# Probabilities times values turned round in a one-core encoder step: split values stationary, split probabilities of 256 queries moving

## What is computed

```python
def sink_attention(q, k, v, bias, mask, sink):            # 8 heads, 2 key/value heads, window of 3 chunks of 64
    s = jnp.einsum('nqkgd,nskd->nkgqs', q, k) * SCALE + bias
    m = jnp.maximum(jnp.max(s, axis=-1, keepdims=True), sk)
    p = jnp.exp(s - m)
    p = p / (jnp.sum(p, axis=-1, keepdims=True) + jnp.exp(sk - m))
    return jnp.einsum('nkgqs,nskd->nqkgd', p, v)

def fox_attend(q, k, v, cq, ck, q_pos, k_pos):            # 8 heads, causal, c = cumsum(log sigmoid(forget logits))
    s = jnp.einsum('bqhd,bshd->bhqs', q, k) * SCALE + cq[..., :, None] - ck[..., None, :]
    s = jnp.where(k_pos[None, :] <= q_pos[:, None], s, NEG)
    return jnp.einsum('bhqs,bshd->bqhd', jax.nn.softmax(s, axis=-1), v)

def merge_and_ffn(x, ya, yb, ga, gb, w_oa, w_ob, w_out, g_ffn, w_gu, w_down):
    merged = jax.nn.sigmoid(ga) * (ya @ w_oa) + jax.nn.sigmoid(gb) * (yb @ w_ob)
    x = x + merged @ w_out
    a, u = jnp.split(rmsnorm(x, g_ffn) @ w_gu, 2, axis=-1)
    return x + (jax.nn.silu(a) * u) @ w_down
```

## Time and profile before

| | us |
|---|---|
| median of three runs | 1628.39 |
| span of the profiled execution | 1626.6 |
| sliding-window stage | 115.9 to 344 |
| forgetting stage | 344 to 607 |
| sample units | 607 to 721 |
| merge and w_out, group 0 | 721 to 812 |
| the rest | 812 to 1626.6 |

### The profile page before, as it was taken

The page is one execution under the profiler, slowest core; times in us unless marked ns, Lnnn a source line. Parts: engine busy times, 40 slices in busy tenths (PEclk is TensorE's granted clock), DMA queues, the critical chain, the costliest instruction groups (busy, mean ns, idle before and its releaser), DMA issues.

```text
span 1626.6 us, 27813 instructions
## 1 busy us (share of the span) xinstructions
PE 1600.6 (98%) x10614; PEld 1507.4 (93%) x10614; DVE 1021.5 (63%) x2232; ACT 665.0 (41%) x1333; POOL 175.3 (11%) x312
## 2 busy tenths in 40 slices
PE   8999999999999999999999999999999999999997
PEld 8999999999999999988898899999999999888886
DVE  6646555655546554436366677776677777679865
ACT  6335444544445444334253552222222223434453
POOL 3011111000000001012011000000121222110000
PEclk9999999999999999999999999999999999999999
DMA  7152332553341425759455332332344444776432
GB/s 210 29 168 95 128 105 68 186 172 93 119 146 52 123 93 152 218 171 326 146 172 193 123 93 93 107 105 75 91 149 157 158 158 165 253 235 187 143 128 87
DMA packets 190292, 230.60 MB, mean 142 GB/s; under 512 B 14808, under 2 KB 140281, under 8 KB 189641
## 3 DMA queue, kind: packets, MB, share of 16 engines
q1 hardware_dynamic: 163616, 138.71, 28.9%
q0 software_dynamic: 26544, 90.12, 15.6%
HBM read 166.76 MB, written 62.08 MB: 141 GB/s over the span
## 4 chain that ended last, share of the span: by engine, by line
PE 91%; DVE 6%; issue 2%; ACT 1%; DMA 1%; SPq 0%; DVEq 0%; ACTq 0%
PE ps L2261 25%; PE ps L2262 24%; PE ps L2263 24%; PE ps L2371 6%; PE ps L2326 3%; PE ps L2344 3%; PE ps L2565 1%; PE ps L2564 1%; DVE sprob L1560 1%; PE ps L2390 1%; DVE e_lo L1911 1%; PE ps L2409 0%; PE ps L2397 0%; PE ps L2283 0%; PE ps L2383 0%
## 5 line engine op out<-in xcount | busy, mean ns | idle before, releaser
L2261 PE MATMUL ps<-h_hi,w_hi 128*128 128x384 f32 (+1 forms) x816 | 274.1, 336 | 1.4 <-DVE h_lo L1532 1.4
L2263 PE MATMUL ps<-h_hi,w_lo 128*128 128x384 f32 (+1 forms) x816 | 266.3, 326 | 0.0
L2262 PE MATMUL ps<-h_lo,w_hi 128*128 128x384 f32 (+1 forms) x816 | 266.2, 326 | 0.0
L2261 PE MATMUL ps<-t_hi,e_hi 128*128 128x272 f32 x704 | 202.7, 288 | 0.9 <-DVE silu L1926 0.9
L2262 PE MATMUL ps<-t_lo,e_hi 128*128 128x272 f32 x704 | 202.8, 288 | 0.0
L2263 PE MATMUL ps<-t_hi,e_lo 128*128 128x272 f32 x704 | 202.1, 287 | 0.0
L2261 PEld LDWEIGHTS ps<-h_hi,w_hi 128*128 128x128 f32 x816 | 153.6, 188 | 3.5 <-DVE h_lo L1532 1.6
L2261 PE MATMUL ps<-b_hi,e_hi 128*128 128x272 f32 x528 | 152.5, 289 | 2.3 <-DVE silu L1926 1.1
L2262 PEld LDWEIGHTS ps<-h_lo,w_hi 128*128 128x128 f32 x816 | 153.5, 188 | 0.5 <-issue 0.5
L2263 PEld LDWEIGHTS ps<-h_hi,w_lo 128*128 128x128 f32 x816 | 153.2, 188 | 0.0
L2262 PE MATMUL ps<-b_lo,e_hi 128*128 128x272 f32 x528 | 152.1, 288 | 0.0
(11 more groups left out here) (340 smaller groups left out, 3620.9 us busy)
## 6 DMA issues: line engine op xcount, KB each, us to landing
w_raw<-in_w_gu_dram SPq DMA_DIRECT2D x104, 256.0 KB, 3.4
w_raw<-in_w_in_dram SPq DMA_DIRECT2D x68, 256.0 KB, 3.3
zg_d<-stg POOLq DMA_DIRECT2D x28, 544.0 KB, 3.0
act_d<-act POOLq DMA_DIRECT2D x44, 272.0 KB, 2.7
s_d<-s_sum POOLq DMA_DIRECT2D x44, 256.0 KB, 3.0
f_raw<-s_d SPq DMA_DIRECT2D x44, 256.0 KB, 2.8
f_raw<-act_d SPq DMA_DIRECT2D x33, 256.0 KB, 2.9
w_raw<-in_w_out_dram SPq DMA_DIRECT2D x32, 256.0 KB, 3.5
```

The source lines that it names most:

```text
L2261: nc.tensor.matmul(out, l_hi, r_hi, start=start, stop=False)
L2262: nc.tensor.matmul(out, l_hi, r_lo, start=False, stop=False)
L2263: return nc.tensor.matmul(out, l_lo, r_hi, start=False, stop=stop)
```

## The change

In `outputs` the operands change sides. The values of a block become the stationary one, high and low part side by side in 128 columns (`va_stack`, `vb_stack`). The turned probabilities become the moving one, high and low part in two products, for two units at once (a **duo**): in the sliding window the two heads of a pair, in the forgetting stage two neighbouring tiles of one head, which is why units 72 to 135 are now ordered by head (`head_start`) and keys, queries, forget sums and values are loaded and split per head. The result lies turned already, rows 0 to 63 of the high values, 64 to 127 of the low values; it is copied by ScalarE (`outputs_out`) and stored to `o_d`, a DMA per duo. Nothing is normalised in the stream: the row sums are kept, inverted once per stage, turned, stored (`rinv_a_d`, `rinv_b_d`) and loaded as rows broadcast over partitions. At the merge's load, per 128 columns of a group's half, VectorE adds the two row halves, multiplies by 1/sum, ScalarE casts and VectorE subtracts. The sample units keep the old form. The sink's exponential is now taken once for all units.

Step n on ScalarE is exp(n+1), evacuation, high part of **all** groups of n, high parts of turned and new things, copy of the duo's outputs (even n); on VectorE the rest of all groups of n, scores(n+2), low parts. TensorE sends outputs of units n-3 and n-2 at odd steps n. Cut to its core (new buffers' places, renamed semaphores and the per-head loads are left out):

```diff
-            def outputs(n):
...
-                for blk, val in enumerate(u["v"]):
-                    K = val.shape[0]
-                    p0 = turned_at(u) + blk * R
-                    last = nc.tensor.matmul(ps[0:R, out_bank(n), 0:w], probT[0:K, p0:p0 + R], val, start=blk == 0, stop=blk == nb - 1)
+            def outputs(m):
+                u, w = units[2 * m], units[2 * m + 1]
+                R, bank = u["rows"], out_bank(m)
+                hi, lo = turned_parts(u)
+                pe.wait_ge(pt_lo, w["group1"])
+                if m >= 2:
+                    pe.wait_ge(ot_evac, m - 1)
...
+                for blk, val in enumerate(w["v"]):
+                    K = val.shape[0]
+                    x0 = 0 if blk < len(u["v"]) else 1
+                    out = ps[:, bank, R * x0:2 * R].rearrange("p (x r) -> p x r", r=R)
+                    nc.tensor.matmul(out, val, hi[0:K, blk, x0:2, 0:R], start=blk == 0, stop=False)
+                    last = nc.tensor.matmul(out, val, lo[0:K, blk, x0:2, 0:R], start=False, stop=blk == len(w["v"]) - 1)
+                last.then_inc(o_ready, 1)
...
+            def turned_hi_part(n):                       # ScalarE
+                for g in range(u["group0"], u["group1"]):
+                    a.wait_ge(pt_ready, g + 1)
+                    for hi, _, src in group_views(u, g):
+                        ins = nc.scalar.copy(hi, src)
+                    ins.then_inc(pt_hi, 1)
+            def outputs_out(m):
+                a.wait_ge(o_ready, m + 1)
...
+                nc.scalar.copy(ost[:, m % 2, 0:w], ps[:, out_bank(m), 0:w]).then_inc(ot_evac, 1)
+            def merged_in_hi(g, part, k):
+                a.wait_ge(sem("ab_scaled"), 4 * (2 * g + part) + k + 1)
+                nc.scalar.copy(rooms[g][("ab_a", "ab_b")[part]][:, 0, k, 0:w], rooms[g][f"raw{part}"][:, 1, k, 0:w])
...
+            def turned_lo_part(n):                       # VectorE
+                for g in range(u["group0"], u["group1"]):
+                    v.wait_ge(pt_hi, g + 1)
+                    for hi, lo, src in group_views(u, g):
+                        ins = nc.vector.tensor_tensor(lo, src, hi.bitcast(F32), ALU.subtract)
+                    ins.then_inc(pt_lo, 1)
+            def merged_in_scale(g, part, ks_):
...
+                for k in ks_:
+                    nc.vector.tensor_tensor(raw[:, 1, k, 0:w], raw[:, 1, k, 0:w], raw[:, 0, k, 0:w], ALU.add)
+                for x, k in enumerate(ks_):
+                    nc.vector.tensor_tensor(raw[:, 1, k, 0:w], raw[:, 1, k, 0:w], r[:, k, 0:w], ALU.mult)
+            def merged_in_lo(g, part, k):
...
+                nc.vector.tensor_tensor(dst[:, 1, k, 0:w], rooms[g][f"raw{part}"][:, 1, k, 0:w], dst[:, 0, k, 0:w].bitcast(F32), ALU.subtract)
...
             for n in range(N_STREAM):                    # VectorE
-                empty_groups(v, nc.vector.tensor_copy, 1, units[n])
+                turned_lo_part(n)
...
-                if n >= 1:
-                    normalise(n - 1)
...
                 evac(d + 1)                              # ScalarE, sample unit s = 3
+                    for k in range(2, 4):
+                        merged_in_hi(0, 0, k)
+                    for k in range(4):
+                        merged_in_hi(0, 1, k)
                 evac(d + 2)
...
                 normalise(N_STREAM + s)                  # VectorE, sample unit
+                if s == 3:
+                    merged_in_scale(0, 1, (0, 1, 2, 3))
+                    for k in range(4):
+                        merged_in_lo(0, 1, k)
...
             def out_first():                             # VectorE; ScalarE has merged_in_hi after each split_hi
+                def chunk(c):
+                    split_lo(b + c + 1, (c + 1) % 2)
+                    merged_in_scale(1, c // 4, (c % 4,))
+                    if c:
+                        merged_in_lo(1, (c - 1) // 4, (c - 1) % 4)
```

More of the change, by code:

```diff
@@ L109 @@
 N_UNITS = 140
+N_SWA = 72
+N_DUOS = N_STREAM // 2
 def rows_of(t):
@@ L116, in pair_start, with head_start @@
 def pair_start(p):
-    return 18 * p if p < 4 else 72 + 16 * (p - 4)
+    return 18 * p
+def head_start(h):
+    return N_SWA + 8 * h
 def is_tok(n):
@@ L148, in bank_of, with out_bank, stat_col @@
     return p % 4 if p < 8 else p % 2
-def out_bank(n):
-    return 1 if n < N_STREAM and n % 2 else 6
+def out_bank(m):
+    return 1 if m % 2 else 6
+def stat_col(u):
+    return 18 * u["pair"] + 9 * u["e"] + u["t"] if u["kind"] == "swa" else u["n"]
 def product_bank(name, f):
@@ new lines, in load_pair, with load_head, load_keys_queries @@
+                saved_block(B_QA + p)
+                load_twice(qz[s], B_QA + p, slice(0, T), f"q_landed{s}")
+            def load_head(dst, n, e, name):
+                saved_block(n)
+                for half in range(2):
+                    sp.dma_start(dst[64 * half:64 * half + 64, :], zg_d[n, 64 * e:64 * e + 64, 0:SEQ]).then_inc(sem(name), 16)
+            def load_keys_queries(h):
+                s, i, e = h % 2, h // 2, h % 2
+                sp.wait_ge(s_ready, units[pair_start(3) - 1 if h == 0 else head_start(h - 1) - 1]["piece1"])
+                load_head(kz[s], B_KB + i, e, f"k_landed{s}")
+                load_head(qfz[s], B_QB + i, e, f"q_landed{s}")
@@ L1099, in turned_hi @@
+            def merged_in_hi(g, part, k):
+                w = 512 if part else GROUPS[g][3]
+                a.wait_ge(sem("ab_scaled"), 4 * (2 * g + part) + k + 1)
+                nc.scalar.copy(rooms[g][("ab_a", "ab_b")[part]][:, 0, k, 0:w], rooms[g][f"raw{part}"][:, 1, k, 0:w]) \
+                    .then_inc(sem("ab_hi"), 1)
             def turned_hi(ev):
-                if ev[0] == "tok":
+                if ev[0] in ("tok", "rinv"):
                     return
                 a.wait_ge(misc_ready, turn_index[ev] + 1)
-                if ev[0] == "ot":
-                    u = units[ev[1]]
-                    R, t, p = u["rows"], u["t"], u["pair"]
-                    if p and t in (0, 4):
-                        a.wait_ge(sem(f"ab_saved{t // 4}"), 32 * p)
-                    ins = nc.scalar.copy(ot_hi[:, P * t:P * t + R], ps[:, 7, 0:R])
-                elif ev[0] == "cache":
+                if ev[0] == "cache":
@@ L1197, in _ @@
             exp(0)
+            a.wait_ge(sem("s_prep_evac"), 3)
+            a.wait_ge(sem("swa_cache_landed"), 32)
+            for rows, blocks in ((slice(0, P), slice(0, NPT + 1)), (slice(0, DEC), slice(NPT + 1, NPT + 2))):
+                nc.scalar.copy(va_stack[rows, blocks, :, 0:HD], va_tok[rows, blocks, :].rearrange("p j (k d) -> p j k d", k=2)) \
+                    .then_inc(sem("v_hi_done"), 1)
             evac(16)
@@ L1205, in _ @@
                     evac(p)
-                empty_groups(a, nc.scalar.copy, 0, units[n])
+                turned_hi_part(n)
                 for ev in turns_at[n]:
@@ L1585, in normalise @@
-                if u["kind"] == "new":
-                    for h in range(2):
-                        rows = slice(64 * h, 64 * h + 64)
-                        ins = nc.vector.tensor_scalar(o_tok[rows, tl, 0:HD], ps[rows, 6, HD * h:HD * h + HD], rinv[rows, c],
-                                                      None, ALU.mult)
-                else:
-                    ins = nc.vector.tensor_scalar(o_tok[0:R, tl, HD * e:HD * e + HD], ps[0:R, out_bank(n), 0:HD], rinv[0:R, c], None,
-                                                  ALU.mult)
@@ L2368, in outputs, with outputs_new @@
+            def outputs_new(s):
+                u = units[N_STREAM + s]
+                for g in range(u["group1"] - 2, u["group1"]):
+                    pe.wait_ge(*emptied(g))
+                if s:
+                    pe.wait_ge(o_evac, s)
+                else:
+                    pe.wait_ge(ot_evac, N_DUOS)
+                pe.wait_ge(sem(f"vc_landed{s % 2}"), 32 * (s // 2 + 1))
                 for blk, val in enumerate(u["v"]):
                     K = val.shape[0]
-                    p0 = turned_at(u) + blk * R
```

587 lines of the change are left out of this document (352 added, 235 removed).

## The result

The changed kernel takes **1615.97 us** (1614.44 to 1616.70, four runs) against 1628.27 for the kernel before beside it: a ratio of 0.9921, with a 95% interval of 0.9907 to 0.9935. It is faster, by 12.3 us, where 40.4 were forecast, and it lies outside the range of 1573 to 1608. The profiled execution took 1614.44 us, its span 1612.5, which is 14.1 less than the 1626.6 of the span before.

What follows compares the result with a forecast made beforehand. TensorE was taken to bound the kernel (busy 98% of the span). Gains of 54.1 us less losses of 13.7 gave 40.4 us off, so a span of 1586.2 and a predicted 1588 us, range 1573 to 1608.

Steps and rivals of the forecast that it cites:

- The products: TensorE, sliding-window and forgetting stages: fp32r products of paired units cost 53.2 us instead of 89.5, gaining 36.3 us.
- Rival 4: TensorE's new products are slower than the score products, e.g. 0.2 us per wide one: 1618 us; chance 0.04.
- The turned outputs: TensorE, sliding-window and forgetting stages: 68 output transposes go, two of 1/sum come, gaining 8.3 us.
- the vanished wait: TensorE no longer waits for an output transpose's bank to empty before turning key or value tiles: 9.5 us gained.
- relay: Per-unit chain through ScalarE and VectorE (exp, evacuation, high copy, rest, scores): loses 3 us in forgetting, 1 in sliding window.
- start: Sliding-window start: ScalarE puts two copies of the values ahead of one evacuation, losing 0.5 us (0 to 1.5).
- cache tiles: Cache tiles turned in steps 130, 132, 133, 134, and first sample scores ahead of last outputs: 1 us lost (0 to 2).
- the mark of a wrong prediction: Signs named beforehand: wide products over 0.13 us apart, TensorE standing over 1 us a head, or pre-merge pause over 9 us.
- The join: Before merge(0): half b's loads land hidden, but the last evacuation stands behind four high copies; 5.2 us lost (3 to 9).
- The clock: TensorE after the stop before merge(0): a slower clock costs 1.5 us (0 to 2.8).
- Group 1's loads: GpSimd's queue carries 6.8 MB instead of 4.6 beside w_out's late weight chunks: 1.5 us lost (0 to 5).
- Rival 2: Loads bound the end: group 0's halves and group 1's loads land late, 5 us each: 1598 us; chance 0.1.

Runs made afterwards that it cites:

- no_sums: The changed kernel without the loads of the sums, so 1/sum is left out of the output: 1604.2 us.
- before_halves: The kernel before, with each load of the merge inputs cut into two DMAs, one per half of the partitions: 1639.9 us.
- combined: The changed kernel with last evacuation before half b's high parts, w_hi behind high copies, outputs loaded into 128 partitions, sums in small loads alternating partition halves: 1594.3 us.

## Why the prediction was wrong, point by point

**The products: right.** Of the 456 fp32r products 440 stand between 116 and 566 us and the last pair's 16 behind, and wide ones start 0.12 us apart, after 0.17 for the first of a unit:

```profile
519.89 0.33 PE L2571 MATMUL ps<-pb_hi,vb_stack 128*128 128x256 f32 x1
520.06 0.28 PE L2572 MATMUL ps<-pb_lo,vb_stack 128*128 128x256 f32 x1
520.18 0.28 PE L2571 MATMUL ps<-pb_hi,vb_stack 128*128 128x256 f32 x1
```

Added up from start to start, the products cost 90.8 us before (89.5 in the prediction, whose 27 for the 272 passes of the first stage should be 26.5 by its own row; they measure 28.2) and 54.2 for the 440 after; with the last 16 at the same price the gain is 34.7 us, where 36.3 were forecast. The narrow ones came at 0.115 each, for the 0.11 taken. Rival 4 is out.

**The turned outputs and the vanished wait: right.** No wait of the key and value turns (L2605, L2607) is left in the groups of 116 to 566 us, and the sliding-window stage came out at 204.6 us for the 203 named; its gross terms, 11.3 + 4.7 + 9.5 = 25.5, less the measured 23.5, leave 2.0 lost, for 1.5 forecast (relay 1, start 0.5).

**The relay: right in kind, too small.** The forgetting stage took 244.8 us instead of 237: 28.6 gross less 18.2 is 10.4 lost, for 4 forecast with the cache tiles. The loads of VectorE and ScalarE were read rightly (143.6 and 145.9 us busy, for 142 and 152). The loss lies between the named ends of 0 and 16, and TensorE stood for more than the 1 us a head that I had set as the mark of a wrong prediction: 8.5 us of waits in eight heads, 12.1 from start to start. The step that failed is the averaging: I put w_hi at 1.4 us into the sum of a head and took a stall of 0.4 for the rest. But it is one item of 1.04 us, and in the units where it comes, it stands ahead of the copy that empties one of two banks. Moving it gave 6.2 us; what is left of the 10.4, 4.2, is near the 4 that I had forecast.

**The join: the order right, the landing wrong.** VectorE came to half b at 678.3 us; by the prediction 720.1 less the 41.7 gained, 678.4. The evacuation behind four high copies costs 5.0 us (a stop of 5.6 in no_sums, less the 0.6 that the kernel before had), for 5.2 forecast. What failed is "landed 15 us after issue, hidden". I took the rate of the earlier trace rows, 2 MB in 9.8 us, for loads of another shape. They landed 22.0 us after the first issue, 5.8 after VectorE got there, and TensorE's stop was 5.8 us longer than by the order alone (11.4 against 5.6); the pause passed the 9 us named as wrong.

**The clock: right after this stop, left out after the later ones.** The stop had a granted clock of 0.67 on average; the first products of merge(0) after it:

```profile
690.74 0.63 PE L2466 MATMUL ps<-ab_a,w_hi 128*128 128x512 f32 x1
691.16 0.63 PE L2467 MATMUL ps<-ab_a,w_lo 128*128 128x512 f32 x1
```

They start 0.43 us apart instead of 0.23, half speed (the 1.2 GHz level), for some six products: 1.3 us, for 1.5 forecast. The rule of the Trainium skill that the prediction cites, "TensorE: Matmul & The Clock Gate", section "HAM oscillation — how this bites in real kernels", is borne out in kind: after this stop the next products ran at half clock. The upper end of 2.8 us at which the prediction put the cost by it was not reached. The prediction had one stop only; w_out has three more, of 4.77, 1.14 and 4.78 us, and the clock after them was put at nothing.

**Group 1's loads: the term that was mis-sized, and the largest.** 1.5 us (0 to 5) were forecast and 15.7 came. Of these 10.7 are waits for w_lo, and the other 5.0 go with slower products (the three lines' means are 424, 412 and 408 ns instead of 389), since after its long stops TensorE runs at half clock (0.50 from 745 to 750 us and 0.66 from 770 to 775; 0.91 over the stage). Rival 2, "the loads bound the end", was the right one, at a chance of 0.1, with its price for w_out again too small (5 us for each place; at the join the landing cost 5.8): it counted 2.2 MB more and not that all 6.8 MB go at about 60% of the rate. before_halves shows the width alone, with 4.6 MB, to be worth 10.2 us in this place. Not all of the 15.7 is width: combined, where the outputs go into 128 partitions and the sums take the halves in turn, still loses 6.2 there. The argument against that rival, "asked for 15 us or more ahead", was about latency, where the question was throughput: loads that fill the engines delay whoever shares them.

The sum again with what was measured: 54.1 - 2.0 - 10.4 - 10.7 - 1.2 - 15.7 = 14.1, the 14.1 of the spans. The 2.0 and the 10.4 are what the gross gain of each stage leaves over, so the sum closes by its making; that the gross gain stood within 2 us is shown by the products added up above. The losses were 40 us instead of 13.7.

## What to carry to other kernels

When a change re-shapes a transfer, price it by its own shape: count the partitions that each DMA writes and its outermost dimension, and take the rate from a row of such a load, not from the megabytes of another. Where the DMA engines are near full, ask whose loads share them; a wait in order for one landing may be harmless while the bytes are not, even when the chain names it. And in a strict queue put work with slack (a weight split, a load's unpacking) behind the copy that frees a bank, since a mean load of an engine hides what one item costs at the wrong place.

## What the runs showed of the hardware that was not expected

- Loads into 64 partitions hold all 16 DMA engines full at 206 GB/s (2 KB packets) or 237 to 254 GB/s (mixed with other loads), where 128 partitions gave 325 to 412. Small ones that take the halves in turn reached 303 GB/s at 93% from SyncE's queue, but 274 at 104% from GpSimd's.
- A load whose outermost dimension is 2 ran on 13.0% of the engines, at 50 GB/s, from SyncE's queue; from GpSimd's it did not stay there.
- Reading one DRAM row for 64 partitions costs no more than reading 64 rows (226 and 223 GB/s while the sums load).
- TensorE's clock can fall after the engine has started again. In combined it stood for 2.71 us, did four products at full rate, and then fell to half (granted clock by stretch, 736 to 739, 739 to 740 and 740 to 743 us), which cost another 1.5 us or so:

```profile
736.00:739.00 3.00, 0.29 (x3) 0.06 (x1) 1.34 (x2) 1.62 (x2) 0.00 (x0) 1.00 1.04 417
739.00:740.00 1.00, 1.00 (x5) 0.82 (x6) 0.97 (x2) 0.00 (x0) 0.00 (x0) 1.00 1.01 414
740.00:743.00 3.00, 3.00 (x9) 2.32 (x8) 1.99 (x3) 1.62 (x2) 0.00 (x0) 0.51 1.05 306
```
